# Up product of an MLP by seven products over half of its depth, and the last blocks in another order with three weighed on GpSimd

## The reference

```
x = x + merged @ w_out
f = rmsnorm(x, norm2_w) @ w_up          # 1024 -> 4096
x = x + square(relu(f)) @ w_down        # 4096 -> 1024
y = rmsnorm(x, norm_f_w)
```

## Time and profile before

| | us |
|---|---|
| median of 3 runs (1617.06 to 1617.59) | 1617.1 |
| profiled execution | 1616.81 |
| its span, first to last instruction | 1615.1 |
| PE busy | 1600.1 (99%) |
| DVE busy | 1059.5 (66%) |
| POOL busy | 720.7 (45%) |
| ACT busy | 530.9 (33%) |

### The profile page before, as it was taken

The page is one execution under the profiler, slowest core; times in us unless marked ns, Lnnn a source line. Parts: engine busy times, 40 slices in busy tenths (PEclk is TensorE's granted clock), DMA queues, the critical chain, the costliest instruction groups (busy, mean ns, idle before and its releaser), DMA issues.

```text
span 1615.1 us, 25413 instructions
## 1 busy us (share of the span) xinstructions
PE 1600.1 (99%) x9776; PEld 1483.0 (92%) x9776; DVE 1059.5 (66%) x1411; ACT 530.9 (33%) x1044; POOL 720.7 (45%) x594
## 2 busy tenths in 40 slices
PE   9999999999999999999999999999999999999997
PEld 8999999999998888999988989999999999999996
DVE  7685977859612221356433587877777887787777
ACT  6655665555522221332134411111111111111123
POOL 5212121121222111223687486666666776666661
PEclk9999999999999999999999999999999999999999
DMA  4201112011184767363354111110011111111012
GB/s 165 68 27 55 54 40 68 27 41 54 41 283 149 233 221 238 118 232 104 122 189 144 53 53 52 53 53 26 27 53 53 52 53 53 53 53 53 27 40 111
DMA packets 133491, 144.99 MB, mean 90 GB/s; under 512 B 7839, under 2 KB 98619, under 8 KB 133372
## 3 DMA queue, kind: packets, MB, share of 16 engines
q1 hardware_dynamic: 133226, 143.34, 27.5%
q10 hardware_dynamic: 146, 0.04, 0.0%
HBM read 124.37 MB, written 18.98 MB: 89 GB/s over the span
## 4 chain that ended last, share of the span: by engine, by line
PE 85%; DVE 9%; ACT 3%; issue 1%; DMA 0%; DVEq 0%; ACTq 0%
PE ps L1289 51%; PE ps L1623 6%; PE ps L1625 6%; PE ps L1624 6%; DVE sp L2114 2%; PE ps L1580 2%; PE ps L1585 2%; PE ps L1583 2%; PE ps L1483 2%; DVE zc L2106 1%; PE ps L1439 1%; PE ps L1449 1%; PE ps L1527 1%; PE ps L1495 1%; ACT sp L1797 1%
## 5 line engine op out<-in xcount | busy, mean ns | idle before, releaser
L1289 PE MATMUL ps<-xh,wh 128*128 128x352 f32 (+1 forms) x956 | 322.6, 337 | 0.9 <-DVE xl L2087 0.7
L1289 PE MATMUL ps<-xh,wl 128*128 128x352 f32 (+1 forms) x956 | 312.7, 327 | 0.0
L1289 PE MATMUL ps<-xl,wh 128*128 128x352 f32 (+1 forms) x956 | 312.4, 327 | 0.0
L2243 DVE TENSOR_TENSOR x<-ps,x 128x1024 f32<-128x1024 f32 x210 | 257.1, 1224 | 42.8 <-PE ps L1625 23.9
L1140 POOL CAST wh<-raw 128x1024 fp32r<-128x1024 f32 x48 | 50.3, 1047 | 478.3 <-issue 205.4
L1289 PE MATMUL ps<-yh,wl 128*128 128x384 f32 (+1 forms) x768 | 250.6, 326 | 0.0
L1289 PE MATMUL ps<-yh,wh 128*128 128x384 f32 (+1 forms) x768 | 250.6, 326 | 0.0
L1289 PE MATMUL ps<-yl,wh 128*128 128x384 f32 (+1 forms) x768 | 250.3, 326 | 0.0
L1921 ACT ACTIVATE hf<-hf 128x384 f32<-128x384 f32 (+1 forms) x96 | 48.6, 508 | 554.7 <-DVE hf L2296 554.7
L1289 PEld LDWEIGHTS ps<-xh,wh 128*128 128x128 f32 x956 | 179.8, 188 | 17.2 <-issue 15.5
L1289 PEld LDWEIGHTS ps<-xl,wh 128*128 128x128 f32 x956 | 180.0, 188 | 0.7
(11 more groups left out here) (213 smaller groups left out, 3141.8 us busy)
## 6 DMA issues: line engine op xcount, KB each, us to landing
raw<-in_w_in SPq DMA_DIRECT2D x80, 256.0 KB, 3.3
cache<-in_cache_k SPq DMA_DIRECT2D x64, 256.0 KB, 3.7
cache<-in_cache_v SPq DMA_DIRECT2D x64, 256.0 KB, 3.5
raw<-in_w_up SPq DMA_DIRECT2D x64, 256.0 KB, 5.4
raw_d<-in_w_down SPq DMA_DIRECT2D x30, 512.0 KB, 4.1
raw<-in_w_out SPq DMA_DIRECT2D x48, 256.0 KB, 2.9
gates<-gst SPq DMA_DIRECT2D x16, 544.0 KB, 6.2
gb<-gates SPq DMA_DIRECT2D x16, 544.0 KB, 5.7
```

Of the source, the lines that this page charges most:

```text
L1289: ins = mm(out, lhs[:, k * P:(k + 1) * P], rhs[:, x], start=(first and a == 0 and m == 0), stop=(last and a == n - 1 and m == 2))
L2243: V_.tensor_tensor(x, src, x, ALU.add).then_inc(step_free, 1)
```

## The change

The up product of pairs 1 to 15 is split by depth. Over depth blocks 4 to 7 it stays direct. Over depth blocks 0 to 3 the two tiles of hidden channels, the two halves of that depth and the two halves of the prompt rows (`HS` = 512) are the blocks of a two by two product, done with seven products. The nine steps of a pair are called `mix` 0 to 8. A product p takes 2 depth blocks with three matmuls each, 512 columns; `over` is the direct half, 4 depth blocks. The 64 sample columns are no longer part of a chunk: `samples(0)` at the end of `mix` 1 and `samples(1)` as `mix` 8 compute them alone, 8 depth blocks with three matmuls each.

Intermediate sums of PSUM banks are kept: `keep` copies a bank to SBUF on ScalarE while later products go on adding to it, and `join` adds the kept copy to a bank on VectorE, after which ScalarE takes relu and square as two operations. The combinations of y are formed once (`twist`, `twist_low`), from float32 copies `y_plain` that VectorE writes as it turns y. For `up` of pair 0, depth blocks 0 to 3 are cut where the tiles of y end (`y_pieces`). The weights of a pair come as one load (`load_pair`), and GpSimd makes six operands of 512 columns out of it with four combinations (`up_op`), in the same ring of five slots as the down operands. `sum` keeps two buffers in place of four. `FINAL` has block 8 second, and blocks 1, 3 and 5 are `away`: GpSimd multiplies by `norm_f_w`, ScalarE by the norm.

Placement of tiles in memory is left out below, as are edits that only rename.

```diff
-        FINAL = (0, 1, 2, 3, 8, 4, 5, 6, 7)
+        FINAL = (0, 8, 1, 2, 3, 4, 5, 6, 7)
...
-                 ("relu", 0, 1), ("relu", 1, 1)]
+                 ("up", 1, 2), ("relu", 1, 0), ("twist",), ("up", 0, 1), ("relu", 1, 2), ("twist_low", 0), ("twist_low", 1),
+                 ("up", 1, 1), ("relu", 0, 1), ("twist_low", 2), ("relu", 1, 1), ("twist_low", 3)]
...
+        MIX_BANK = {"x": 4, "y": 5, "z": 6, "w": 0, "few": 1}
+        MIX = [("x", 0, None), ("y", 1, (0, 0)), ("z", 3, None), ("x", 2, None), ("z", 5, (0, 1)), ("x", 4, None), ("w", 6, (1, 0)),
+               ("x", None, (1, 1))]
+        KEEP = {0: (0, 0), 2: (1, 1), 3: (0, 1), 5: (1, 0)}
+        JOIN = {1: (0, 0), 4: (0, 1), 6: (1, 0), 7: (1, 1)}
+        W_PART = {0: (0, 0), 1: (0, 1), 3: (2, 0), 2: (2, 1), 5: (3, 0), 4: (3, 1), 6: (4, 1)}
+        W_PLAIN = (1, 5)
+        W_FEW = (0, 4)
+        U_LAST = (1, 4, 3, 5, 8, 8)
+        RELU_NO = {1: 1, 4: 2, 6: 3, 7: 4}
+        KEPT_FOR = {3: 1, 4: 2, 5: 3, 7: 4}
+        TWIST_NO = {3: 0, 4: 1, 2: 2, 6: 3}
+        TWIST_OF = (3, 4, 2, 6)
+        TWIST_IN = ((0, 0), (0, 1), (1, 1), (1, 0))
 
...
+            m = n - 1
+            tail += [("sum", m, 0), ("sum", m, 1), ("mix", n, 0), ("keep", n, 0), ("prep", m, 0), ("prep", m, "few0"), ("prep", m, "few1"),
+                     ("mix", n, 1), ("mix", n, 2), ("keep", n, 2), ("mix", n, 3), ("keep", n, 3), ("join", n, 1),
+                     ("prep", m, 1), ("prep", m, 6), ("mix", n, 4), ("mix", n, 5), ("keep", n, 5), ("prep", m, 3), ("prep", m, 4),
+                     ("join", n, 4), ("sum", m, 2), ("mix", n, 6), ("prep", m, 2), ("join", n, 6), ("sum", m, 3),
+                     ("mix", n, 7), ("prep", m, 5), ("join", n, 7), ("mix", n, 8), ("join", n, 8)]
...
         for k, b in enumerate(FINAL):
-            if b != FINAL[-1]:
-                tail += [("block", b, 0), ("block", b, 1)]
-                if k:
-                    tail.append(("final", FINAL[k - 1]))
-            else:
-                tail += [("block", b, 0), ("final", FINAL[k - 1]), ("final_half", b, 0), ("block", b, 1), ("final_half", b, 1)]
+            if b == FINAL[-1]:
+                tail += [("block", b, 0), ("square", FINAL[k - 1]), ("half_square", b, 0), ("away", FINAL[k - 2]), ("block", b, 1),
+                         ("half_square", b, 1), ("half", b), ("final", FINAL[k - 1]), ("final", b)]
+                continue
+            tail += [("block", b, 0), ("block", b, 1)]
+            if k:
+                tail += [("square", FINAL[k - 1]), ("final", FINAL[k - 1])]
+            if b == NB:
+                tail.append(("low_move", b))
+            if k > 1:
+                tail.append(("away", FINAL[k - 2]))
...
             if p == 0 and q == 0:
-                return read_no["up", 2 * n + 3, 1]
+                return read_no["mix", n + 1, 8]
...
 
-            return read_no["up", 2 * n + 3, 2] if h == 0 else read_no["prod", n, 5, 1]
+            return read_no["mix", n + 1, 8] if h == 0 else read_no["prod", n, 5, 1]
...
                 else:
-                    sp_.wait_ge(n_turned, NB + 1)
+                    sp_.wait_ge(twist_lo, 4)
...
+            def load_pair(n):
+
+                if n == 1:
+                    sp_.wait_ge(w_split, 6 * NPAIR + 3 * KT + 2 + N_OUT + 2)
+                else:
+                    sp_.wait_ge(d_lo, ring_no["u", n - 1, len(U_LAST) - 1] + 1)
...
-                        load_tile(N_OUT + u)
+                if n + 2 < N_TWIN:
+                    load_pair(n + 2)
...
+            def twist(out, one, other, op):
+
+                g.tensor_tensor(out, one, other, op).then_inc(t_made, 1)
+                turns[0] += 1
+                pool.wait_ge(t_made, turns[0])
+
+            def slot_free(of):
+
+                if of < 2:
+                    pool.wait_ge(step_done, tile_end["up", 0])
+                elif of < N_RING:
+                    pool.wait_ge(step_done, tile_end["up", 1])
+                else:
                     pool.wait_ge(step_done, op_used(of - N_RING))
+                if of == N_RING - 1:
+                    pool.wait_ge(twist_lo, 4)
                 apart(pool)
...
+                s1, s2, s4, s3 = (blocks(tw[t])[:, KQ * h:KQ * h + KQ, :] for t in range(2) for h in range(2))
+                of = ring_no["u", n, x]
+                if x == 0:
+                    pool.wait_ge(u_in, 32 * n)
+                slot_free(of)
+                if x == 2:
+                    twist(s1, a21, a22, ALU.add)
+                    twist(s2, s1, a11, ALU.subtract)
+                elif x == 3:
+                    twist(s3, a11, a21, ALU.subtract)
+                    twist(s4, a12, s2, ALU.subtract)
+                src = (rows_[:, 0:KT // 2, 0:P], rows_[:, KT // 2:KT, 0:P], blocks(tw[0]), blocks(tw[1]),
+                       rows_[:, 0:KT // 2, P:2 * P], rows_[:, KT // 2:KT, P:2 * P])[x]
+                split_op(of, src, blocks)
...
+                for x in range(len(U_LAST)):
+                    up_op(n + 1, x)
+                for k in range(N_OP):
+                    if n == LAST_TWIN - 1 and k >= N_SOON:
                         end_low(k - N_SOON)
                     down_op(n, k)
-                if 2 * n + 5 < 2 * N_TWIN:
-                    tail_tile(N_OUT + 2 * n + 5)
+
+            pool.wait_ge(wf_in, 16)
+            for k, b in enumerate(AWAY):
+                if k >= 2:
+                    pool.wait_ge(y_scaled, k - 1)
+                pool.wait_ge(step_free, read_no["block", b, 1])
+                apart(pool)
+                g.tensor_tensor(weighed[k][:, :], x1[:, b * D:(b + 1) * D], wfb[:, :], ALU.mult).then_inc(y_weighed, 1)
...
-                                      first=half == 0, last=half == 1)
+                    pe.wait_ge(step_free, step_no["up", j, c] + 1)
+                    pe.wait_ge(y_lo, 6 * [p for p in range(3) if PASSES[p][0][0] == 3 * c][0] + 6)
+                    order_ = [*range(KT // 2, KT), *range(KT // 2)]
+                    for f in order_:
+                        pieces = y_pieces(f, a, z)
+                        for piece in pieces:
+                            out = bank(up_bank(j, c), piece[0] - a, piece[1] - a)
+                            for m, (w, part) in enumerate(((wh, 0), (wh, 1), (wl, 0))):
+                                ins = mm(out, w[n % 2][:, f * P:(f + 1) * P], y_at(f, part, *piece), start=(f == order_[0] and m == 0),
+                                         stop=(f == order_[-1] and m == 2), skip_group_check=True)
...
+                    def three(out, w, y, start, stop):
+
+                        for t, (high, part) in enumerate(((0, 0), (0, 1), (1, 0))):
+                            ins = mm(out, w[high], y[part], start=start and t == 0, stop=stop and t == 2, skip_group_check=True)
+                        return ins
...
+                    def samples(i):
+
+                        out = bank(MIX_BANK["few"], i * SMP, (i + 1) * SMP)
+                        for f in range(KT):
+                            x, q = (W_FEW[i], f) if f < KT // 2 else (W_PLAIN[i], f - KT // 2)
+                            ins = three(out, weight(x, q), [y_at(f, part, SEQ, NTOK) for part in range(2)], f == 0, f == KT - 1)
+                        return ins
+
+                    if m < len(MIX):
+                        where, p, over = MIX[m]
+                        out = bank(MIX_BANK[where])
+                        if m in (3, 4, 5, 7):
+                            pe.wait_ge(kept, 4 * (n - 1) + KEPT_FOR[m])
+                        else:
+                            pe.wait_ge(step_free, mix_bank_read(n, m))
+                        begun = where == "x" and m > 0 or (where == "z" and m > 2)
+                        if over:
+                            i, j = over
+                            pe.wait_ge(d_lo, ring_no["u", n, W_PLAIN[i]] + 1)
+                            for f in range(KT // 2, KT):
+                                ins = three(out, weight(W_PLAIN[i], f - KT // 2), [y_at(f, part, j * HS, (j + 1) * HS) for part in range(2)],
+                                            not begun and f == KT // 2, p is None and f == KT - 1)
+                            begun = True
+                        if p is not None:
+                            x, h = W_PART[p]
+                            pe.wait_ge(d_lo, ring_no["u", n, x] + 1)
+                            if n == 1 and p in TWIST_NO:
+                                pe.wait_ge(twist_lo, TWIST_NO[p] + 1)
+                            for q in range(KQ):
+                                ins = three(out, weight(x, KQ * h + q), [y_op[p][part][:, q * HS:(q + 1) * HS] for part in range(2)],
+                                            not begun and q == 0, q == KQ - 1)
+                        if m == 1:
+                            ins = samples(0)
+                    else:
+                        pe.wait_ge(d_lo, ring_no["u", n, W_FEW[1]] + 1)
+                        ins = samples(1)
```

(118 more changed lines are left out.)

217 lines of the change are left out of this document (104 added, 113 removed).

## The result

The changed kernel takes 1718.86 us (median of 4 runs, 1717.65 to 1721.1) where the kernel before takes 1617.08 beside it: 1.063 times as long, 95% interval 1.0618 to 1.0643. The prediction was 1680, in a range up to 1702. Slower was right; the size was not, by 39 us.

A forecast was written before the change was run, and what follows sets the result against it. TensorE, issuing without a pause, was taken as the bound. From 1616.8 us, +61 for 15 pairs (2.05 samples, 2.0 wait each), +4.8 pair 0, +1.2 last pair and -3.6 end gave 1680, range 1648 to 1702.

The forecast's parts named there:

- The new wait before `prod` 0: In each of 15 pairs `prod` 0 waits for `join` 8: a stall of 2.0 us, bounds 0.65 to 3.
- Sample matmuls, +2.05 a pair: Up part, 15 times: 48 separate sample matmuls at 0.111 us, a weight load's spacing, make it 25.76 against 23.71 us.
- cheap-samples rival: Sample matmuls cost 0.040 us each, while VectorE's row still delays `prod` 0: about 1654 us, chance 0.08.
- the faster one: Rival: short matmuls cost only their columns and VectorE's row and GpSimd fit in: 1594 us, chance 0.04.
- The row of 11.7 us: From the end of `mix` 5 to `join` 8, ScalarE and VectorE alternate: 11.7 us by mean durations, taken as 11.5.
- GpSimd: Splits and combinations in each pair keep GpSimd busy about 45 us, under the pair's 48.7, so it adds nothing.
- The rival in which it binds: GpSimd bounds each pair: three quarters of its work disturbed, 50 us with slot waits, 1700 us; chance 0.14.
- Pair 0: Once, in the first pair: cut chunks cost 3.4 us and the wait of `mix` 0 about 1.4, together +4.8.
- The last pair: Once: GpSimd first makes down operands 3 and 4, so it is late for `few` 1: +1.2 us (0 to 4).
- The end, -3.6: At the kernel's end VectorE's lag falls from 4.6 us to about 1: -3.6 us (-4.5 to 0).

The follow-up runs named there:

- the cut version: The changed kernel with sample products in PSUM bank 7 and only 2 of their 8 depth blocks computed: 1629.0 us, ratio 1.0073.
- alone: The kernel before with only the changed order of final blocks and three of them weighed on GpSimd, MLP untouched: 1614.04 us, ratio 0.9977.
- the bank 7 version: The changed kernel with a pair's sample products in PSUM bank 7 in place of bank 1, all matmuls kept: 1658.0 us, ratio 1.0255.

## Why the prediction was right in kind and wrong in size

**The step that failed** is "The new wait before `prod` 0". Its length was right: "a stall of 2.0 us a pair" against 2.25. What it left out is what follows the wait. The step prices the matmuls of the down part at 20.92 as before ("The down part's matmuls don't change"), and with the clock at half for `prod` 0 they take 23.15. That is 15 x 2.1 = 32 us of the 39 missing for the clock, and 2 for the 0.12 that stays without a wait; 4 more are the wait's last quarter of a microsecond, 2 are pair 0, and the 1.2 forecast for the last pair is not paid. The trace of before could have warned: in its last 34.20 us, where TensorE waits, the granted clock is 0.88. I read the busy times from that row and not the clock.

**Sample matmuls, +2.05 a pair.** Right: 25.74 and 25.76 against 25.76, and 0.112 for one by the cut version. The cheap-samples rival and the faster one both needed 0.04 to 0.07 and fall.

**The row of 11.7 us.** 11.3 measured, but by two errors that cancel. I had put the sums in the row at 1.42 and 1.34; they take 1.19 and 0.68 there and run beside ScalarE. In their place stand relu and square on ScalarE, 1.3 a turn, ahead of each high part, which I had left out.

**GpSimd.** It never holds a pair of the changed kernel up: 37.97 us busy in a pair where I had 45. Combinations of up weights are 256 columns wide and take 0.73, where I took 1.36. The rival in which it binds came nearest to the time, at 1700, by a mechanism that isn't there.

**Pair 0.** +6.9 against 4.8. TensorE waits 2.67 us before the first `mix` for a read that stands behind a `twist_low` of 1.82 us on VectorE, where I had 1.4.

**The last pair.** In the changed kernel GpSimd is done in time, since `prod` 0 to 6 are later by the wait and by the clock. It is a wait of 3.44 us as soon as these go, as the bank 7 version shows; the term was real and covered by a larger one.

**The end, -3.6.** Right to 0.1 us, in the changed kernel and alone.

Left open: why the clock falls in some pairs and not in others at the same gap, and whether thin matmuls or the pair's length make it fall in every pair of the changed kernel. The runs show how often, not by what rule.

## What to carry to other kernels

A wait of TensorE can have two prices: its length and, here mostly from gaps of 2.1 us on, the matmuls behind it at the lower clock; so look at the granted clock in stretches, the idle ones of the kernel before among them, before pricing one. When matmuls are merged or cut, ask first what becomes of the short ones that rode along, since each still needs its weight load. A result that only VectorE's last step can give should not stand in the bank that TensorE wants next: a free bank was worth 61 us here.
